# DeltaNet stage of a hybrid trunk: chunks prepared for both directions from one set of scores, decay rows fetched in a deeper ring, second inverse begun before the recurrence

## The chip, the core and the metric

One Trainium2 chip, one core of it. The engines in the profile are PE (TensorE), DVE (VectorE), ACT (ScalarE), POOL (GpSimd) and SP (SyncE, which here only issues DMAs); ACT also issues DMAs, from the same queue of instructions as its arithmetic. The metric is the device time of one execution in microseconds, the median of several runs.

## The reference, cut to what matters

One layer of a trunk with four branches, cross attention and a mixture of experts over 1024 tokens of width 1024. The change lies in branch D, the bidirectional gated DeltaNet with 4 heads of width 64:

```
def gdn_scan(q, k, v, beta, log_a):
    ...
    gam = jnp.cumsum(gc, axis=-1)
    diff = gam[..., :, None] - gam[..., None, :]
    ...
    decay = jnp.exp(jnp.where(incl, diff, -jnp.inf))
    kk = jnp.einsum('bhntd,bhnsd->bhnts', kc, kc)
    a_mat = jnp.where(strict, bc[..., None] * kk * decay, 0.0) + jnp.eye(c, dtype=jnp.float32)
    rhs = jnp.concatenate([vc * bc[..., None], kc * (bc * jnp.exp(gam))[..., None]], axis=-1)
    sol = lax.linalg.triangular_solve(a_mat, rhs, left_side=True, lower=True, unit_diagonal=True)
    u_val, k_cum = sol[..., :dv], sol[..., dv:]
    qk = jnp.einsum('bhntd,bhnsd->bhnts', qc, kc) * decay
    ...
    def step(state, inp):
        u_i, kc_i, qk_i, qd_i, kd_i, cd_i = inp
        v_new = u_i - jnp.einsum('bhtd,bhde->bhte', kc_i, state)
        o = jnp.einsum('bhtd,bhde->bhte', qd_i, state) + jnp.einsum('bhts,bhse->bhte', qk_i, v_new)
        state = cd_i[..., None, None] * state + jnp.einsum('bhsd,bhse->bhde', kd_i, v_new)
        return state, o
...
    o_f = gdn_scan(q, k, v, beta[:, :, 0], log_a[:, :, 0])
    o_b = _flip(gdn_scan(_flip(q), _flip(k), _flip(v), _flip(beta[:, :, 1]), _flip(log_a[:, :, 1])))
```

The scan runs once forward and once backward. The products of keys with keys and of queries with keys inside one chunk do not depend on the direction; the decays and the write strengths beta do.

## The kernel before

The kernel works in chunks of 128 tokens, TT = 8 of them. One list, `schedule` (made in `plan_schedule`), orders the work of all engines. Every engine walks the same list and carries out its own part of each step, so the list fixes each engine's order, and semaphores hold the engines together. `dense` lays the parts of the dense projections (a part is six 128x512 matmuls of L800, or twelve of 128x256) into a list of other steps: each `None` in that list is one part. The dense work between the DeltaNet steps belongs to branch 2's merge and the gates of branch 3 (panels `merge20` to `merge23`, `early1`, `early2`, `nz`). With a panel go its conversions (L1355 on ACT, L1971 on DVE) and the evacuations of its groups: a gate group is evacuated by ACT (L1381), an "up" group by DVE (L1994, L2000). Two PSUM banks alternate for them, so a group waits until the group two before it has been evacuated.

DeltaNet is done in two stages, each over eight indices i.

Preparation. Index i stands for chunk i in the forward direction and for chunk 7 - i in the backward one. Part 0: the rows of the summed log decays come back from DRAM (`gdn_rows`, broadcast to 128 partitions, one DMA for each direction, issued by ACT at L1728 two indices ahead), POOL takes the differences and masks them (L2823, L2826), ACT takes the exponential into the buffer that will be written out (L1722). That buffer, `LQ[i % 2]`, must have been written to `gdn_lq` for index i - 2 first, and ACT waits for that. Part 1: PE forms the scores, 8 matmuls for each direction (16 instructions, L997); DVE multiplies decay by beta (L2393) and both by the scores (L2401, twice for each direction). Part 2: ACT copies the diagonal 32x32 blocks aside (L1734, eight small copies), and `gdn_out` issues the write of 1 MB to `gdn_lq` (L1769).

The diagonal blocks of four indices (128 of them: four indices, two directions, four heads, four blocks) are sent to DRAM (`gdn_ship`, L1773), come back with one block in each of 128 partitions (`gdn_read`, L1783), and are inverted there by DVE, one row at a time: 30 rows, each a multiplication (L2413) and a subtraction (L2416), cut into ten steps `gdn_inv` of three rows, called p = 0 to 9 below. L2408 opens it, L2419, L2421 and L2424 close it. There are two such inverses, b = 0 for indices 0 to 3 and b = 1 for 4 to 7. `gdn_back` writes the inverse to DRAM (L1789), `gdn_load_inv` fetches the piece for an index (L1809, four DMAs), and `gdn_load` fetches the prepared matrices (L1799).

Recurrence (`gdn_c`, parts 0 to 6 for each index). POOL spreads the inverse into block diagonals (L2835, four instructions) and scales the keys (L2853, L2855). Two doubling steps complete the triangular inverse: PE L1021, DVE L2434, PE L1030 and L1037, DVE L2439 and L2441, PE L1021, ACT L1753, PE L1037, ACT L1757. Then PE L1044, ACT L1761, PE L1050 and L1058, DVE L2447, PE L1064 to L1072, ACT L1765, DVE L2452 and L2457.

In the list before, five of the ten steps of inverse 0 stand between the preparations of indices 5 to 7 and five after them; all ten steps of inverse 1 stand between the parts of the recurrence for indices 0, 1 and 2. Where a wait of a DMA stands in ACT's queue, everything behind it on ACT waits too, evacuations of gates among it.

## Time and profile before

| | us |
|---|---|
| median of 3 runs | 2031.6 |
| lowest, highest | 2030.33, 2033.76 |
| the profiled execution's own time | 2035.94 |
| its span in the trace | 2034.2 |

PE is busy for 1883.2 us of the span (93%), DVE for 1384.7 (68%), ACT for 1078.3 (53%), POOL for 312.2 (15%); the mean granted clock of TensorE is 0.971 of full speed. The profiled execution's time is 1.7 us above its span and 4.3 us above the median. The preparation, the inverses and the recurrence lie between 676.57 us (first L997) and 954 us (last L1072), 14% of the span. Timeline rows give start, duration, engine, line, operation and in brackets the idle time of that engine ahead of it with what ended it; ACTq is ACT's sequencer issuing a DMA.

### The profile page before, as it was taken

To read this page: it belongs to the slowest core of one execution; us is meant where nothing else is said; L and a number is where in the kernel's file an instruction comes from. 1 tells how busy PE (TensorE), PEld (TensorE's weight loads), DVE (VectorE), ACT (ScalarE), POOL (GpSimd) and SP (SyncE) were. 2 spreads that over 40 slices of the span, in tenths; PEclk is the share of its full clock that TensorE was granted. 3 is DMA by queue.
4 is the path that set the end of the run, shared out by engine and by line. 5 is a ranking of instruction groups with operands and counts; after the bars stand their busy time and mean duration, and the time that the engine had idled before them with its cause. 6 is when DMAs were issued, how large, how long until landed. Compare 5 with 4: busy or idle time off the path is not lost.

```text
span 2034.2 us, 32665 instructions
## 1 busy us (share of the span) xinstructions
PE 1883.2 (93%) x12949; PEld 1118.7 (55%) x12949; DVE 1384.7 (68%) x1833; ACT 1078.3 (53%) x1568; POOL 312.2 (15%) x269
## 2 busy tenths in 40 slices
PE   6999999999999989899999999995899999999991
PEld 3464565655544545677488855684455444444440
DVE  5555533799874797544733745437799999999997
ACT  4563223566646531223433534334588888888873
POOL 6000100344310502241000000000000111111103
PEclk8999999999999999999999999997899999999996
DMA  5411111212011663431621410404799999999987
GB/s 189 162 48 46 32 42 48 73 48 58 22 28 47 198 195 84 146 113 45 212 70 60 158 32 16 169 32 163 279 423 422 422 422 422 422 422 422 423 328 269
DMA packets 145821, 366.83 MB, mean 180 GB/s; under 512 B 39296, under 2 KB 94880, under 8 KB 119072
## 3 DMA queue, kind: packets, MB, share of 16 engines
q1 hardware_dynamic: 96608, 279.57, 36.2%
q10 hardware_dynamic: 40240, 52.50, 7.6%
q0 software_dynamic: 8848, 33.03, 4.3%
q8 instruction: 86, 1.41, 0.3%
q14 instruction: 39, 0.32, 0.0%
HBM read 314.14 MB, written 46.73 MB: 177 GB/s over the span
## 4 chain that ended last, share of the span: by engine, by line
PE 77%; DVE 8%; ACT 5%; issue 4%; DMA 3%; ACTq 1%; SPq 1%; POOL 1%; POOLq 0%; DVEq 0%
PE psum L800 38%; PE psum L1191 24%; ACT arena L1637 2%; PE psum L1180 1%; DMA gdn_lq<-arena 1%; PE psum L1115 1%; PE psum L1090 1%; DVE arena L2314 1%; PE psum L930 1%; PE psum L1209 1%; PE psum L817 1%; ACTq L1809 1%; PE psum L1072 1%; PE psum L1050 1%; DMA arena<-in_w_in_dram 1%
## 5 line engine op out<-in xcount | busy, mean ns | idle before, releaser
L800 PE MATMUL psum<-arena 128*128 128x512 f16 (+2 forms) x6000 | 1017.2, 327 | 18.3 <-ACT arena L1381 6.9
L800 PEld LDWEIGHTS psum<-arena 128*128 128x128 f16 x6000 | 569.1, 99 | 402.0 <-issue 19.2
L1191 PE MATMUL psum<-arena 128*128 128x512 f16 x2304 | 513.6, 382 | 15.2 <-issue 12.2
L751 DVE SCALAR_TENSOR_TENSOR arena<-arena 128x2048 f16<-128x2048 f32 x192 | 437.4, 2286 | 57.0 <-ACT arena L745 56.8
L745 ACT ACTIVATE arena<-arena 128x2048 f16<-128x2048 f32 x192 | 365.4, 1908 | 71.1 <-DMA arena<-in_w_dram 41.9
L1191 PEld LDWEIGHTS psum<-arena 128*128 128x128 f16 x2304 | 224.6, 98 | 282.0 <-issue 24.3
L1971 DVE SCALAR_TENSOR_TENSOR arena<-arena 128x512 f16<-128x512 f32 (+1 forms) x185 | 125.6, 698 | 114.9 <-ACT arena L1355 114.5
L2872 POOL DMA_INDIRECT arena<-xhat,arena x32 | 66.5, 2078 | 841.5 <-PE psum L1180 445.2
L1355 ACT ACTIVATE arena<-arena 128x512 f16<-128x512 f32 (+1 forms) x212 | 127.4, 616 | 53.5 <-PE psum L800 21.7
L1381 ACT ACTIVATE arena<-psum,arena 128x512 f32<-128x512 f32 x60 | 41.0, 684 | 139.4 <-PE psum L800 138.6
L1444 ACT ACTIVATE arena<-psum 128x512 f32<-128x512 f32 (+3 forms) x51 | 29.9, 586 | 127.6 <-PE psum L800 127.6
L1409 ACT ACTIVATE arena<-arena 128x256 f32<-128x256 f32 x64 | 26.7, 416 | 109.8 <-DVE arena L2006 108.7
L2767 POOL TENSOR_SCALAR arena<-arena 128x512 f32<-128x512 f32 x27 | 57.5, 2130 | 137.7 <-ACT arena L1355 137.7
L2299 DVE CUSTOM_DVE_ANT_0 arena<-psum,arena 128x1024 f32<-128x1024 f32 x64 | 75.6, 1219 | 1.8 <-PE psum L917 1.7
L1637 ACT ACTIVATE arena<-arena 128x1024 f32<-128x1024 f32 x64 | 72.9, 1146 | 6.8 <-DVE arena L2299 6.7
L1994 DVE SCALAR_TENSOR_TENSOR arena<-arena,psum 128x512 f32<-128x512 f32 x64 | 43.8, 684 | 43.2 <-PE psum L800 32.2
L2024 DVE SCALAR_TENSOR_TENSOR arena<-psum,arena 128x512 f16<-128x512 f32 x36 | 24.9, 690 | 61.2 <-ACT arena L1444 31.0
L2006 DVE SCALAR_TENSOR_TENSOR arena<-psum,arena 128x512 f32<-128x512 f32 x32 | 22.1, 691 | 65.0 <-PE psum L800 65.0
L1646 ACT ACTIVATE arena<-psum 128x512 f16<-128x512 f32 x64 | 34.7, 595 | 55.1 <-PE psum L930 34.3
L2835 POOL TENSOR_TENSOR arena<-arena 128x512 f32<-128x512 f32 x32 | 34.5, 1110 | 146.4 <-PE psum L1058 94.4
L1886 ACT ACTIVATE arena<-psum 128x512 f32<-128x512 f32 x64 | 38.2, 597 | 15.3 <-PE psum L1191 14.6
L1180 PE MATMUL psum<-arena 128*128 128x128 f32 x256 | 34.5, 279 | 9.4 <-DMA arena<-xhat,arena 9.4
(388 smaller groups left out, 2020.6 us busy)
## 6 DMA issues: line engine op xcount, KB each, us to landing
arena<-in_w_dram SPq DMA_DIRECT2D x192, 1024.0 KB, 11.9
arena<-in_merge_w_dram SPq DMA_DIRECT2D x64, 256.0 KB, 3.2
yrows<-arena ACTq DMA_DIRECT2D x32, 512.0 KB, 7.8
arena<-in_w_in_dram SPq DMA_DIRECT2D x48, 256.0 KB, 2.8
gdn_lq<-arena ACTq DMA_DIRECT2D x8, 1024.0 KB, 4.5
arena<-gdn_lq ACTq DMA_DIRECT2D x8, 1024.0 KB, 4.9
arena<-in_xattn_wkv_dram SPq DMA_DIRECT2D x32, 256.0 KB, 2.9
yrows<-arena POOLq DMA_DIRECT2D x1, 7680.0 KB, 24.1
```

What stands on the lines that cost most here:

```text
L745: nc.scalar.activation(half_of(pieces(e, m)[0], half), half_of(XLAND[m], half), ACT.Copy, scale=WS).then_inc(w_hi[m], 1)
L751: nc.vector.scalar_tensor_tensor(half_of(lo, half), half_of(XLAND[m], half), WS, half_of(hi, half), ALU.mult, ALU.subtract).then_inc(w_lo[ ...
L800: mm = nc.tensor.matmul(bank[prt[0]:prt[1], c0:c1], lhs[a](k), rhs[b](k), start=(k == 0 and a + b == 0), stop=(k == nk - 1 and a == 1))
L1180: tr = nc.tensor.transpose(PS[:, k // 4, (k % 4) * P:(k % 4) * P + P], xs[:, k, :], ident)
L1191: mm = nc.tensor.matmul(PS[:, bank, :], left[a][:, k, :], right[b][:, k, columns], start=k + a + b == 0, stop=(k == n - 1 and a == 1))
L1355: S.activation(W[i % 2][0][:, 2 * j:2 * j + 2, 0:wide], LAND[c % NLAND][:, :, 0:wide], ACT.Copy, scale=WS).then_inc(*act_hi.mark(c))
L1637: S.activation(DS[u % 2][:, m, :], DS[u % 2][:, m, :], ACT.Exp, scale=-1.0, bias=d_mx[u % 2][:, m:m + 1], accum_out=d_l[u % 2][:, m:m + 1])\
L1971: V.scalar_tensor_tensor(W[i % 2][1][:, 2 * j:2 * j + 2, 0:wide], LAND[c % NLAND][:, :, 0:wide], WS, W[i % 2][0][:, 2 * j:2 * j + 2, 0:wid ...
L1994: V.scalar_tensor_tensor(dst, gate, 1.0, bank, ALU.add, ALU.mult).then_inc(*e.mark(n))
L2299: V.tensor_tensor_reduce(out=DS[u % 2][:, m, :], in0=PS[:, 2 + 2 * m:4 + 2 * m, :].rearrange("p a b -> p (a b)"), in1=DWH[:, 896 - P * qt: ...
L2767: G.tensor_scalar(landed_c, landed_c, WS, None, ALU.mult).then_inc(*counter("pool_w_scaled").mark(chunk))
L2872: G.indirect_dma_start(XR[e % 2], None, XH_D, bass.IndirectOffsetOnAxis(IDX[:, e:e + 1], 0)).then_inc(rows_in[e % 2], 16)
```

## The change

An index of the preparation now stands for one chunk in both directions. The order of chunks is CH = 0, 7, 1, 6, 2, 5, 3, 4, so that index i (with i ^ 1 for the other direction) holds what the recurrence's index needs. The scores are formed once for each chunk, and two sets of PSUM banks alternate by i % 2. The rows of both directions come in one DMA of 512 KB for each chunk. The buffers of rows from index 2 on form a ring of three; rows 2 and 3 are issued at the start of index 0, rows j = i + 3 at `gdn_out(i)`, with four semaphores. ACT's exponential works in place in the rows' buffer, so it no longer waits for the write of `gdn_lq`; DVE waits for that write ahead of its first product instead. The 1 MB write is two DMAs of 512 KB. Inverse pieces are grouped by chunk: four DMAs write an inverse where two did, and two DMAs fetch a piece where four did. In the list, p = 0 and 1 of inverse 0 stand in the preparation and p = 2 to 9 behind it; p = 0 to 5 of inverse 1 stand ahead of the recurrence and p = 6 to 9 in its index 0, followed by `gdn_back(1)` ahead of part 6. The `None` entries are set anew: three dense parts for each index of the preparation instead of three or four, and from index 3 of the recurrence on every dense part stands where it stood.

```diff
@@ -260,19 +260,20 @@
     inv = lambda b, p: [("gdn_inv", b, 3 * p + 1, 3 * p + 4)]
     gdn += [("gdn_a", 0, 0), None, None, None, None]
     for i in range(TT):
-        mid = {6: inv(0, 2)}.get(i, [])
-        gdn += [("gdn_a", i, 1)] + {6: inv(0, 1), 7: inv(0, 4)}.get(i, []) + [None] + [("gdn_a", i + 1, 0), None] * (i + 1 < TT) + mid
-        gdn += [("gdn_a", i, 2), ("gdn_out", i)] + [("gdn_ship", 0)] * (i == 3) + [None]
-        gdn += {4: [("gdn_read", 0), None], 5: inv(0, 0) + [None], 6: inv(0, 3) + [None], 7: [("gdn_ship", 1)]}.get(i, [])
-    for p in range(5, 10):
-        gdn += inv(0, p) + [None] * (2 + (p < 8)) + [("gdn_load", p - 5)] * (p < 7)
-    gdn += [("gdn_back", 0)] + [None] * 6 + [("gdn_load_inv", 0), ("gdn_load_inv", 1), ("gdn_read", 1)] + [None] * 7
+        gdn += [("gdn_a", i, 1), None] + [("gdn_a", i + 1, 0), None] * (i + 1 < TT) + [("gdn_a", i, 2), ("gdn_out", i)]
+        gdn += {3: [("gdn_ship", 0)], 5: inv(0, 0), 6: inv(0, 1), 7: [("gdn_ship", 1)]}.get(i, []) + [None]
+        gdn += {4: [("gdn_read", 0)], 7: [None]}.get(i, [])
+    for p in range(2, 10):
+        gdn += inv(0, p) + [None] * (2 + (p == 9)) + {5: [("gdn_read", 1)], 6: [("gdn_load", 0)], 7: [("gdn_load", 1)]}.get(p, [])
+    gdn += [("gdn_back", 0)]
+    for p in range(6):
+        gdn += inv(1, p) + [None, None] + [("gdn_load_inv", 0), ("gdn_load_inv", 1)] * (p == 2)
     for i in range(TT):
         for part in range(7):
-            gdn += [("gdn_back", 1)] * ((i, part) == (3, 1))
-            gdn += [("gdn_c", i, part)] + [None] * (1 + (i < 3 and part in (1, 4) and (i, part) != (2, 1)))
-            if i < 3 and part in (1, 2, 4) or (i, part) == (0, 5):
-                gdn += inv(1, 3 * i + (i > 0) + (1, 2, 4, 5).index(part))
+            gdn += [("gdn_back", 1)] * ((i, part) == (0, 6))
+            gdn += [("gdn_c", i, part), None] + [None] * (i < 2 and part in (1, 4))
+            if i == 0 and part in (1, 2, 4, 5):
+                gdn += inv(1, 6 + (1, 2, 4, 5).index(part))
             if part == 2 and i and i + 1 < TT:
                 gdn += [("gdn_load", i + 1), ("gdn_load_inv", i + 1)]
...
-        NGR = [[f32(BR + 8192 + 1024 * j + 512 * d, NH, P) for d in range(2)] if j < 2 else (NX, NZ_)[j % 2] for j in range(TT)]
+        NGR = [f32(BR + 8192 + 1024 * j, 2, 512) if j < 2 else f32(UN + 2048, 2, 1536)[:, :, 512 * (j % 3):512 * (j % 3) + 512]
+               for j in range(TT)]
+        NDT = [[m[:, d, :].rearrange("p (h n) -> p h n", h=NH) for d in range(2)] for m in NGR]
+        CH = [c for k in range(TT // 2) for c in (k, TT - 1 - k)]
+        AT = [CH.index(i) for i in range(TT)]
...
-                    for d in range(2):
-                        c = i if d == 0 else TT - 1 - i
-                        cs = slice(c * P, c * P + P)
-                        B0, B1, B2 = (PS[:, 2 + 3 * d + b, :].rearrange("p (h n) -> p h n", h=NH) for b in range(3))
-                        if part == 1:
-                            if i == 0 and d == 0:
-                                pe.wait_ge(*counter("act_gdnp").at("tm", "nv", 3))
-                                pe.wait_ge(*counter("act_gdnp").at("egrows"))
-                            if i:
-                                pe.wait_ge(*v.at("qt", i - 1, d))
-                            for t in range(4):
-                                for u, bank in enumerate((B1, B2)):
-                                    hp = slice(64 * u, 64 * u + 64)
-                                    mm = nc.tensor.matmul(bank[:, t, :], NK[hp, t % 2, cs], (NK if t < 2 else NQ)[hp, t % 2, cs],
-                                                          start=True, stop=True)
-                                    if t == 3:
-                                        mm.then_inc(*q.mark("qk", i, d, u))
+                    cs = slice(CH[i] * P, CH[i] * P + P)
+                    B1, B2 = (PS[:, 3 + 3 * s + b, :].rearrange("p (h n) -> p h n", h=NH) for b in range(2))
+                    if part == 1:
+                        if i == 0:
+                            pe.wait_ge(*counter("act_gdnp").at("tm", "nv", 3))
+                            pe.wait_ge(*counter("act_gdnp").at("egrows"))
+                        if i >= 2:
+                            pe.wait_ge(*v.at("qt", i - 2, 1))
+                        for t in range(4):
+                            for u, bank in enumerate((B1, B2)):
+                                hp = slice(64 * u, 64 * u + 64)
+                                mm = nc.tensor.matmul(bank[:, t, :], NK[hp, t % 2, cs], (NK if t < 2 else NQ)[hp, t % 2, cs],
+                                                      start=True, stop=True)
+                                if t == 3:
+                                    mm.then_inc(*q.mark("qk", i, u))
...
                     if part == 0:
+                        for j in range(2, 4) if i == 0 else ():
+                            act.wait_ge(*counter("act_gdnp").at("tm", "nv", 3))
+                            S.dma_start(NGR[j], A["gdn_rows"][0].rearrange("(d c h) n -> c d (h n)", d=2, h=NH)[CH[j]].partition_broadcast(P))\
+                                .then_inc(gam_in[j % 4], 16)
                         for d in range(2):
-                            c = i if d == 0 else TT - 1 - i
                             act.wait_ge(*po.at("low", i, d))
-                            after(act, lq_out[i % 2], 16 * (i // 2))
-                            S.activation(NQT[i % 2][d], NGR[i][d], ACT.Exp).then_inc(*a.mark("dt", i, d))
-                        j = i + 2
-                        for d in range(2):
-                            if j < TT:
-                                act.wait_ge(*(a.at("dt", j - 2, d) if j >= 4 else counter("act_gdnp").at("tm", "nv", 3)))
-                                r0 = 32 * d + 4 * (j if d == 0 else TT - 1 - j)
-                                S.dma_start(NGR[j][d], A["gdn_rows"][0, r0:r0 + 4].partition_broadcast(P)).then_inc(gam_in[j % 2], 16)
+                            S.activation(NDT[i][d], NDT[i][d], ACT.Exp).then_inc(*a.mark("dt", i, d))
                     elif part == 2:
...
                     act.wait_ge(*counter("vec_gdn").at("qt", i, 1))
-                    S.dma_start(A["gdn_lq"][i], LQ[i % 2]).then_inc(lq_out[i % 2], 16)
+                    j = i + 3
+                    if 4 <= j < TT:
+                        S.dma_start(NGR[j], A["gdn_rows"][0].rearrange("(d c h) n -> c d (h n)", d=2, h=NH)[CH[j]].partition_broadcast(P))\
+                            .then_inc(gam_in[j % 4], 16)
+                    for d in range(2):
+                        S.dma_start(A["gdn_lq"][i ^ d, :, 1024 * d:1024 * d + 1024], LQ[i % 2][:, 1024 * d:1024 * d + 1024]).then_inc(lq_out[i % 2], 16)
...
                     for n, m in enumerate((NU[b], NUT[b])):
-                        S.dma_start(A["gdn_inv"][b, n].rearrange("u (b f) -> (u b) f", b=4), m.rearrange("p r c -> p (r c)")).then_inc(inv_out[b], 16)
+                        for d in range(2):
+                            S.dma_start(A["gdn_inv"][b, n].rearrange("(k e h) (b f) -> e k (h b) f", e=2, h=NH, b=4)[d],
+                                        m[64 * d:64 * d + 64].rearrange("p r c -> p (r c)")).then_inc(inv_out[b], 16)
...
-                    S.dma_start(LQ[s], A["gdn_lq"][i]).then_inc(lq_in[s], 16)
+                    S.dma_start(LQ[s], A["gdn_lq"][AT[i]]).then_inc(lq_in[s], 16)
                 elif what == "gdn_load_inv":
                     i = step[1]
                     s = i % 2
-                    act.wait_ge(inv_out[i // 4], 32)
+                    b, k = divmod(AT[i], 4)
+                    act.wait_ge(inv_out[b], 64)
                     if i >= 2:
                         act.wait_ge(*counter("pe_gdn").at("o", i - 2, 1))
                     for n in range(2):
-                        for d in range(2):
-                            u0 = 16 * d + 4 * (i % 4)
-                            S.dma_start(XZC[s][:, 8 * n + 4 * d:8 * n + 4 * d + 4, :],
-                                        A["gdn_inv"][i // 4, n, u0:u0 + 4].rearrange("u (p c) -> p u c", c=32)).then_inc(lq_in[s], 16)
+                        S.dma_start(XZC[s][:, 8 * n:8 * n + 8, :],
+                                    A["gdn_inv"][b, n, 8 * k:8 * k + 8].rearrange("u (p c) -> p u c", c=32)).then_inc(lq_in[s], 16)
...
                             if i >= 2:
                                 dve.wait_ge(*a.at("diag", i - 2, d, 3))
-                            V.tensor_tensor(NLT[s][d], NQT[s][d], bc(BES[:, d, c, :].unsqueeze(2), P, NH, P), ALU.mult)\
+                                dve.wait_ge(lq_out[s], 32 * (i // 2))
+                            V.tensor_tensor(NLT[s][d], NDT[i][d], bc(BES[:, d, CH[i], :].unsqueeze(2), P, NH, P), ALU.mult)\
                                 .then_inc(*v.mark("dt1", i, d))
                             dve.wait_ge(*v.last())
-                            BB = PS[:, 3 + 3 * d:5 + 3 * d, :]
+                            BB = PS[:, 3 + 3 * s:5 + 3 * s, :]
                             for u in range(2):
-                                dve.wait_ge(*q.at("qk", i, d, u))
-                            for n, (of, to) in enumerate((("lt", NLT), ("qt", NQT))):
-                                both = to[s][d].rearrange("p (u t) n -> p u (t n)", u=2)
-                                V.tensor_tensor(both, BB[:, :, 256 * n:256 * n + 256], both, ALU.mult).then_inc(*v.mark(of, i, d))
+                                dve.wait_ge(*q.at("qk", i, u))
+                            for n, (of, to, by) in enumerate((("lt", NLT[s][d], NLT[s][d]), ("qt", NQT[s][d], NDT[i][d]))):
+                                to, by = (m.rearrange("p (u t) n -> p u (t n)", u=2) for m in (to, by))
+                                V.tensor_tensor(to, BB[:, :, 256 * n:256 * n + 256], by, ALU.mult).then_inc(*v.mark(of, i, d))
```

ACT's queue in the preparation, from the write at the end of index 0 to the conversion behind index 1's write. L1769 and L1773 are `gdn_out`, L1722 and L1726 the exponential, L1728 and L1770 the fetch of rows, L1734 and L1733 the diagonal copies. Before:

```order
L1769 DMA gdn_lq<-arena 128x2048
L1381 ACTIVATE arena<-psum,arena 128x512
L1722 ACTIVATE arena<-arena 128x512 x2
L1728 DMA arena<-gdn_rows 128x512 x2
L1734 ACTIVATE arena<-arena 32x128 x8
L1769 DMA gdn_lq<-arena 128x2048
L1355 ACTIVATE arena<-arena 128x512
```

Now:

```order
L1773 DMA gdn_lq<-arena 128x1024 x2
L1384 ACTIVATE arena<-psum,arena 128x512
L1726 ACTIVATE arena<-arena 128x512 x2
L1733 ACTIVATE arena<-arena 32x128 x8
L1770 DMA arena<-gdn_rows 128x2x512
L1773 DMA gdn_lq<-arena 128x1024 x2
L1358 ACTIVATE arena<-arena 128x512
```

The fetch of rows moved behind the diagonal copies and stands directly ahead of the two writes.

DVE's queue ahead of the first product of the recurrence (L2434 before, L2438 now). L2421, L2424 close inverse 0; L2417, L2420 are rows of an inverse in the changed kernel. Before:

```order
L2421 TENSOR_SCALAR arena<-arena 128x1024
L2424 MEMSET arena 128x32 x2
L1971 SCALAR_TENSOR_TENSOR arena<-arena 128x512
L1994 SCALAR_TENSOR_TENSOR arena<-arena,psum 128x512
...
L1971 SCALAR_TENSOR_TENSOR arena<-arena 128x512 x2
L1994 SCALAR_TENSOR_TENSOR arena<-arena,psum 128x512
L2000 TENSOR_TENSOR arena<-arena 128x512
L2434 TENSOR_SCALAR arena<-psum 32x4x32 x4
```

Now:

```order
L1976 SCALAR_TENSOR_TENSOR arena<-arena 128x512
L1999 SCALAR_TENSOR_TENSOR arena<-arena,psum 128x512
L2005 TENSOR_TENSOR arena<-arena 128x512
L2417 TENSOR_TENSOR arena<-arena 128x240
L2420 TENSOR_TENSOR arena<-arena 128x15x16
L2417 TENSOR_TENSOR arena<-arena 128x238
L2420 TENSOR_TENSOR arena<-arena 128x14x17
L2417 TENSOR_TENSOR arena<-arena 128x234
L2420 TENSOR_TENSOR arena<-arena 128x13x18
L2438 TENSOR_SCALAR arena<-psum 32x4x32 x4
```

Eighteen rows of inverse 1 now stand between the end of inverse 0 and the first product of the recurrence; the last three are shown.

ACT's queue from the copy ahead of L1050 (L1761 before, L1760 now) in index 0 of the recurrence to the fetch of rows for index 1. Before:

```order
L1761 ACTIVATE arena<-psum 128x256 x2
L1355 ACTIVATE arena<-arena 128x512
L1381 ACTIVATE arena<-psum,arena 128x512
L1765 ACTIVATE arena<-psum 128x256 x2
L1748 DMA arena<-gdn_rows 64x256 x4
```

Now:

```order
L1760 ACTIVATE arena<-psum 128x256 x2
L1384 ACTIVATE arena<-psum,arena 128x512
L1794 DMA gdn_inv<-arena 4x16x1024 x4
L1764 ACTIVATE arena<-psum 128x256 x2
L1747 DMA arena<-gdn_rows 64x256 x4
```

The four writes of inverse 1 now stand ahead of the copies that free the output's bank for index 1.

## Rows read from the trace of the kernel before

**Rows 1.** The chain that ended last: by engine, page.

```profile
PE 77%; DVE 8%; ACT 5%; issue 4%; DMA 3%; ACTq 1%; SPq 1%; POOL 1%; POOLq 0%; DVEq 0%
```

**Rows 2.** Timeline of PE: start, duration, line, idle ahead and its releaser.

```profile
676.57 2.06 PE L997 MATMUL psum<-arena 64*128 64x128 f32 x32
...
717.03 5.35 PE L800 MATMUL psum<-arena 128*128 128x512 f16 x24
...
746.11 28.87 PE L800 MATMUL psum<-arena 128*128 128x512 f16 x126 [6.15 <-DVE arena L1994]
...
802.20 0.60 PE L1021 MATMUL psum<-arena 32*32 32x32 f32 x32
...
805.16 0.34 PE L1030 MATMUL psum<-arena 32*32 32x32 f32 x5 [0.95 <-DVE arena L2434]
...
814.74 1.09 PE L1044 MATMUL psum<-arena 128*64 128x128 f32 x16 [1.07 <-ACT arena L1757]
...
838.42 1.09 PE L1044 MATMUL psum<-arena 128*64 128x128 f32 x16 [2.35 <-ACT arena L1757]
...
861.79 1.98 PE L1044 MATMUL psum<-arena 128*64 128x128 f32 x16 [1.99 <-ACT arena L1757]
```

**Rows 3.** Waits in 665 to 760 us: who, for whom, total, times, longest.

```profile
ACT arena L1722 <- DMA gdn_lq<-arena: 15.2, 6, 3.7
```

**Rows 4.** Stretch, us, busy of PE, PEld, DVE, ACT, POOL; clock, DMA share, GB/s.

```profile
678.64:780.58 101.94, 87.53 (x571) 44.97 (x572) 81.36 (x146) 40.60 (x99) 29.86 (x30) 0.95 0.63 196
850.98:874.62 23.64, 21.66 (x227) 14.75 (x226) 7.24 (x22) 4.88 (x11) 6.41 (x9) 0.93 0.43 134
874.62:894.59 19.97, 19.97 (x227) 13.85 (x227) 9.25 (x25) 4.58 (x10) 7.30 (x9) 1.00 0.49 153
862.00:867.00 5.00, 5.00 (x34) 3.49 (x33) 1.36 (x3) 1.54 (x4) 0.00 (x0) 0.68 0.72 185
```

**Rows 5.** Timeline of DVE.

```profile
663.65 1.29 DVE L1971 SCALAR_TENSOR_TENSOR arena<-arena 128x512 f16<-128x512 f32 x2
...
776.15 2.81 DVE L1971 SCALAR_TENSOR_TENSOR arena<-arena 128x512 f16<-128x512 f32 x2 [6.15 <-ACT arena L1355]
...
780.59 1.24 DVE L2434 TENSOR_SCALAR arena<-psum 32x128 f32<-32x128 f32 x4
...
786.61 1.03 DVE L2408 COPY arena<-arena 64x1024 f32<-64x1024 f32 x1
787.67 0.20 DVE L2413 TENSOR_TENSOR arena<-arena 128x30 f32<-128x30 f32 x1
...
796.20 0.42 DVE L2447 TENSOR_TENSOR arena<-psum,arena 128x256 f32<-128x256 f32 x1 [0.85 <-PE psum L1058]
```

**Rows 6.** DVE: rows of inverse 1 (L2413, then L2416), p = 0 to 5.

```profile
786.61:815.55 28.94, 6.17 (x18) 1.00 0.17 54
786.61:815.55 28.94, 6.21 (x18) 1.00 0.17 54
```

**Rows 7.** DMA issues in 676 to 743 us: KB each, median us to landing.

```profile
gdn_lq<-arena ACTq DMA_DIRECT2D x8, 1024.0 KB, 4.5
arena<-gdn_diag ACTq DMA_DIRECT2D x2, 256.0 KB, 6.6
```

**Rows 8.** Timeline of ACT and its DMA issues (ACTq).

```profile
705.12 1.30 ACT L1734 ACTIVATE arena<-arena 32x128 f32<-32x128 f32 x4 [0.41 <-ACT arena L1722]
...
835.45 2.50 ACTq L1809 DMA_DIRECT2D arena<-gdn_inv  x4
...
852.24 2.21 ACTq L1789 DMA_DIRECT2D gdn_inv<-arena  x2
```

**Rows 9.** Timeline of POOL.

```profile
773.94 4.48 POOL L2835 TENSOR_TENSOR arena<-arena 128x512 f32<-128x512 f32 x4 [52.05 <-DMA arena<-gdn_inv]
...
794.91 4.04 POOL L2835 TENSOR_TENSOR arena<-arena 128x512 f32<-128x512 f32 x4 [13.30 <-PE psum L1058]
803.08 0.61 POOL L2853 TENSOR_TENSOR arena<-arena 128x256 f32<-128x256 f32 x1 [4.14 <-DVE arena L2457]
```

30 lines of the change are left out of this document (14 added, 16 removed).

## The prediction

> **What bounds the kernel now.** I read the chain of work that ended last first: PE holds 77% of it [rows 1], so a wait of PE is lost unless PE waits again later for the same thing. Then the timeline of PE, from the first scores at 676.57 us to the recurrence's index 4 at 874.62. PE's large wait is the 6.15 us at 746, for an evacuation by DVE; in the recurrence it waits 0.95 us for DVE and 1.07, 2.35 and 1.99 us for ACT's L1757 [rows 2]. Third, the list of waits: in the preparation ACT waits 15.2 us in six waits for writes to gdn_lq, with evacuations of gates queued behind [rows 3]. That is what the in-place exponential removes. Fourth, busy time by stretch: between DVE's first product of the preparation (678.64) and its first of the recurrence (780.58), DVE is busy for 81.36 of 101.94 us and PE for 87.53 [rows 4]. So DVE has only some 20 us of room there, and the change moves 18 rows of inverse 1 into it. From index 4 of the recurrence on PE has no idle time (19.97 busy of 19.97 us, rows 4), so what is gained by then reaches the end.
>
> **The scores.** 128 of 256 instructions of L997 go. 32 of them stand in 2.06 us [rows 2], so 8 x 1.0 = 8 us of PE's work goes. I cost it at nothing: it lies ahead of the first product of the recurrence, and there DVE comes last, as the next part shows. If DVE were early, it would be worth up to 8 us.
>
> **When DVE reaches the recurrence.** Everything DVE does before L2434 remains: 81.36 us busy [rows 4]. Of it I take off 1.5 us, the lengthening of two L1971 (2.81 us for two, against 1.29 without POOL beside them, rows 5) that I count again under POOL. The 60 instructions of inverse 0 leave gaps of 0.03 us each (786.61 + 1.03 to 787.67, rows 5): 1.8 us. The moved steps p = 0 to 5 are 6.17 + 6.21 us of rows [rows 6] and 1.03 us of L2408 [rows 5], with 37 such gaps: 14.5 us. Without a wait DVE arrives at 678.64 + 81.36 - 1.5 + 1.8 + 14.5 = 774.8.
>
> Waits in the preparation: the write of index i - 2 now holds DVE instead of ACT. A write lands 4.5 us after its issue [rows 7]; a fetch of rows of 512 KB is now issued right ahead of it, and diagonal copies of 1.30 us stand ahead of both [rows 8]. DVE's own work on the index between, about 4.4 us plus conversions, covers most of that. What is not covered is the conversion on DVE (L1971), which needs ACT's L1355, which stands behind the last diagonal copies (1.3 us) and three issues. Walking the two queues index by index, I find DVE idle for 2.1, 1.2 and 1.2 us ahead of three conversions, and 0.9 us for the first inverse's blocks, which need 6.6 us to land [rows 7]: 5.4 us. Bounds 0 (writes and conversions all covered) and 14 us (each of six indices also waits 1.5 us, because the write shares the DMAs with the rows in front of it). DVE then arrives at 780.2.
>
> POOL: the four L2835 and the four scalings of keys for index 0 now run while DVE works on inverse 1. Their length is 4 x 1.01 (4.04 for four) + 4 x 0.61 = 6.5 us [rows 9]. The nearest row is the pair of L1971 at 776.15: beside POOL's L2835 until 778.42 it took 2.81 us instead of 1.29, 1.52 us lost in 2.27 us of POOL [rows 5, 9], a share of 0.67. Rows of an inverse read two operands from SBUF as L1971 does, and about 85% of DVE's instructions there are such: 6.5 x 0.67 x 0.85 = 3.7 us. Bounds 0 and 6.5. I take 3.7 since the row is the same kind of instruction beside the same line. The Trainium skill ("SBUF — State Buffer", Who interferes with whom) says that a DVE instruction with two SBUF inputs and a GpSimd instruction that reads SBUF exclude each other, and that the later one blocks until the other's end. By that rule it would be nearer 6.5; it speaks against this change, and is weighed as a rival.
>
> So DVE reaches the recurrence at 783.9, 3.3 us later than before (780.59, rows 5), and PE's L1030 waits for it. PE's own work to that place is 87.53 - 8 + 1.3 (a part more, below) = 80.8 us, so that it could be there from 759.5 on, and inverse 0, which the first product needs, ends earlier than before. **Term 1: +3.3 us.**
>
> **The recurrence.** Term 2: one dense part that stood in indices 0 to 2 now stands ahead, where PE has room. Four parts take 5.35 us [rows 2]: -1.3 us.
> Term 3: indices 0 to 2 hold p = 6 to 9 instead of all ten. The 0.95 us for DVE goes. The waits for L1757 (1.07, 2.35) come from ACT issuing four L1809, 2.50 us for four [rows 8]; two are left, 1.2 us less, and in index 2 a gate's evacuation no longer stands right ahead of them. I keep 0.4: -4.0 us. Bounds -4.4 and -1 (if an issue of twice the blocks takes twice as long).
> Term 4: p = 9 and the end of inverse 1 (3.6 us, an estimate: three short pairs of rows and two instructions of the size of L2408) stand on DVE behind L2447 of index 0, and on ACT the four writes of `gdn_back(1)` wait for it, ahead of the copies L1765 (L1764 now) that free PE's bank for index 1. From POOL's L2835 of index 1 (794.91, when PE's L1058 is done) to index 1's start (802.20) there were 7.3 us. Now: 1.7 to the end of L2447 (796.20 + 0.42, rows 5), 3.6, issues of 2.0 (0.4 to 1.1 each: 2.21 for two at 852.24, rows 8) and copies of 0.8: 8.1, a wait of 0.9 (0.8 rounded up for the gaps). POOL's L2835 stands beside it for 2.2 us more: 1.4. +2.3 us, bounds 0 and 5.
> Term 5: index 3 took 23.64 us where index 4 took 19.97 [rows 4] with the same work. 1.99 us were the wait for L1757, and the rest the clock, 0.68 granted in the 5 us behind that wait. With 1.2 us fewer issues most of the wait goes; -2.0, bounds 0 and -3.6.
>
> Sum: +3.3 - 1.3 - 4.0 + 2.3 - 2.0 = -1.7 us. The profiled execution would take 2035.94 - 1.7 = 2034.2, and the median 2031.6 - 1.7 = 2029.9. The profiled run lay 4.3 us above the median, so only the difference is carried over.
>
> **Rivals.**
> A, POOL costs nothing and DVE enters early. For it: DVE's products from PSUM beside POOL keep their length. Then 3.7 and 1.4 us go from terms 1 and 4: -6.8, 2024.8. With the preparation's waits at 0 too it would be -12.2, 2019.4.
> B, slower: DVE and POOL exclude each other fully. Place: p = 3 to 5 ahead of the recurrence and the end of inverse 1. Price: 2.8 more in term 1, 2.6 more in term 4, and after some 5 us of waiting PE's clock stays low for a while as in index 3: 1.6. -1.7 + 7.0 = +5.3, 2036.9. (The rule of the Trainium skill named above is this rival.) It decides from about 0.95 us lost for each us of POOL, together with that clock. Against it: the measured share is 0.67.
> C, the writes: each of the six indices from 2 on waits 1.5 us more behind the 512 KB of rows, +9 less what other waits hide (1.3): -1.7 + 7.7 = +6.0, 2037.6. Against it: the DMA engines were 63% busy over the stretch [rows 4], so there is room.
> D, the change doesn't fetch earlier: rows j = i + 3 are issued behind the copies of index i, where rows i + 3 stood just ahead of them before. POOL's wait stays, ACT's exponential comes late, +2: 2031.9. POOL's work for an index (4 x 1 us) starts two indices ahead, which speaks against a cost.
>
> **How the numbers follow.** The measurement can tell about 0.2%, 4.1 us, from no change. The forecast has a chance of 0.40, with a range of its own of 2025.5 to 2034.5; of it 0.10 is faster by more than that, 0.25 within, 0.05 slower. A has 0.34 (0.27 faster, 0.07 same), B 0.14 (0.11 slower, 0.03 same), C 0.08 (0.06 slower, 0.02 same), D 0.04 (same). Faster 0.37, same 0.41, slower 0.22. The range runs from A's far half to B and most of C: 2020.5 to 2037.5.
>
> **What would show it.** In the profile after: ACT's wait for gdn_lq is gone and DVE has one; the last product of the preparation ends near 732 by the same walk; DVE's first product of the recurrence starts at 784 (A: 780 or less, B: 787), with PE waiting for it; L2835 lies beside rows that take longer than 0.4 us; PE waits about 2 us at index 1's start and hardly for L1757; index 4 starts at 873. It is wrong if PE reaches the recurrence later than DVE, or if the waits in the preparation pass 10 us.

## The result, and the profile after

The changed kernel takes 2046.96 us (median of 6 runs, 2045.52 to 2048.83) against 2032.68 for the kernel before in the same comparison. The ratio is 1.0071, 95% interval 1.0056 to 1.0086: 14 us slower, where the prediction said 2029.9 and a range of 2020.5 to 2037.5.

The profiled execution of the kernel after took 2045.59 us, span 2043.8, granted clock 0.971. PE still holds the chain (78%, where [rows 1] had 77%), so the loss has to be found as waits of PE. First its timeline, to be laid beside [rows 2]: start, duration, line, idle ahead and its releaser. L1000 are the scores (L997 before), L1024 the start of an index of the recurrence (L1021), L1033 the product that waits for DVE (L1030).

```profile
676.24 1.16 PE L1000 MATMUL psum<-arena 64*128 64x128 f32 x16
...
722.62 2.74 PE L805 MATMUL psum<-arena 128*128 128x512 f16 x6 [5.64 <-ACT arena L1384]
...
772.88 7.93 PE L805 MATMUL psum<-arena 128*128 128x512 f16 x30 [3.86 <-ACT arena L1384]
786.15 5.54 PE L805 MATMUL psum<-arena 128*128 128x512 f16 x18 [5.33 <-ACT arena L1384]
...
795.10 0.34 PE L1033 MATMUL psum<-arena 32*32 32x32 f32 x5 [1.48 <-DVE arena L2438]
...
815.68 0.71 PE L1067 MATMUL psum<-arena 128*128 128x128 f32 x4 [2.77 <-DVE arena L2451]
...
825.00 0.71 PE L1024 MATMUL psum<-arena 32*32 32x32 f32 x32 [2.61 <-issue]
...
849.12 0.60 PE L1024 MATMUL psum<-arena 32*32 32x32 f32 x32
...
869.19 0.60 PE L1024 MATMUL psum<-arena 32*32 32x32 f32 x32
...
890.14 0.60 PE L1024 MATMUL psum<-arena 32*32 32x32 f32 x32
```

The first scores stand at 676.24 (676.57 before), index 4 at 890.14 (874.62 before): 15.5 us are lost in between, and the split is clean. DVE's first product of the recurrence comes at 794.43 instead of 780.59 [rows 5]: +13.8. From there to index 1's start it is 825.00 - 794.43 = 30.57 us, where it was 802.20 - 780.59 = 21.61: +9.0. Indices 1 to 3 take 890.14 - 825.00 = 65.14 us instead of 72.42: -7.3. Of the 30.57 us PE works for 24.49, at a granted clock of 0.89, where it worked for all of the 21.61 at full clock: 6.1 of the 9.0 us are PE standing idle and 2.9 are matmuls lengthened by the lower clock (columns: us, busy of PE, PEld, DVE, ACT, POOL, granted clock, share of the 16 DMA engines, GB/s; first the kernel before, then the kernel after, then a part of it and one of the groups made longer).

```profile
780.59:802.20 21.61, 21.61 (x204) 14.40 (x202) 17.55 (x46) 4.93 (x11) 5.05 (x6) 1.00 0.12 36
```

```profile
794.43:825.00 30.57, 24.49 (x200) 16.26 (x201) 22.34 (x54) 4.08 (x10) 6.74 (x8) 0.89 0.09 26
816.00:820.00 4.00, 4.00 (x24) 4.00 (x23) 3.63 (x13) 0.00 (x0) 0.00 (x0) 0.57 0.01 4
```

```profile
816.84 1.81 PE L1075 MATMUL psum<-arena 128*128 128x64 f32 x8
```

What lies behind index 4 is not changed; it measures between 1153.7 and 1160.4 us from execution to execution of all the kernels here, which is why the two profiled spans differ by 9.6 and the medians by 14.3.

Where do the 13.8 us come from? DVE's timeline (as rows 5), with every wait of over half a us between the first product of the preparation (678.48) and the recurrence:

```profile
689.76 0.69 DVE L1976 SCALAR_TENSOR_TENSOR arena<-arena 128x512 f16<-128x512 f32 x1 [0.85 <-ACT arena L1358]
...
696.45 0.90 DVE L1976 SCALAR_TENSOR_TENSOR arena<-arena 128x512 f16<-128x512 f32 x1 [2.15 <-ACT arena L1358]
...
704.39 0.69 DVE L1976 SCALAR_TENSOR_TENSOR arena<-arena 128x512 f16<-128x512 f32 x1 [1.29 <-ACT arena L1358]
...
714.16 0.69 DVE L1976 SCALAR_TENSOR_TENSOR arena<-arena 128x512 f16<-128x512 f32 x1 [4.46 <-ACT arena L1358]
...
723.75 1.03 DVE L2412 COPY arena<-arena 64x1024 f32<-64x1024 f32 x1 [3.27 <-DMA arena<-gdn_diag]
...
749.46 0.69 DVE L1999 SCALAR_TENSOR_TENSOR arena<-arena,psum 128x512 f32<-128x512 f32 x1 [0.93 <-PE psum L805]
...
786.71 0.99 DVE L1976 SCALAR_TENSOR_TENSOR arena<-arena 128x512 f16<-128x512 f32 x1 [4.43 <-ACT arena L1358]
...
789.07 1.24 DVE L2417 TENSOR_TENSOR arena<-arena 128x240 f32<-128x240 f32 x1
790.34 1.13 DVE L2420 TENSOR_TENSOR arena<-arena 128x240 f32<-128x240 f32 x1
791.50 0.70 DVE L2417 TENSOR_TENSOR arena<-arena 128x238 f32<-128x238 f32 x1
...
794.43 1.24 DVE L2438 TENSOR_SCALAR arena<-psum 32x128 f32<-32x128 f32 x4
```

The waits shown make 17.4 us; with three short ones (0.18, 0.38, 0.23) it is 18.2. Without POOL beside it a row of this length takes about 0.4 us; at 789 to 790 two take 1.24 and 1.13, the next four 0.7 each. The next timeline, of ACT and its DMA issues (ACTq) and of POOL, shows who was waited for at 782 to 787, and again at 825:

```profile
709.74 2.71 ACTq L1770 DMA_DIRECT2D arena<-gdn_rows  x1
...
766.99 5.04 ACTq L1794 DMA_DIRECT2D gdn_inv<-arena  x4
772.14 0.69 ACT L1384 ACTIVATE arena<-psum,arena 128x512 f32<-128x512 f32 x1 [10.40 <-DVE arena L2420]
...
783.03 2.28 ACTq L1814 DMA_DIRECT2D arena<-gdn_inv  x4
785.40 0.69 ACT L1384 ACTIVATE arena<-psum,arena 128x512 f32<-128x512 f32 x1 [12.06 <-issue]
...
819.49 4.98 ACTq L1794 DMA_DIRECT2D gdn_inv<-arena  x4
824.52 0.38 ACT L1764 ACTIVATE arena<-psum 128x256 f32<-128x256 f32 x1 [16.15 <-issue]
```

```profile
786.12 5.09 POOL L2839 TENSOR_TENSOR arena<-arena 128x512 f32<-128x512 f32 x4 [64.68 <-DMA arena<-gdn_inv]
```

The four writes of the inverse are issued in 5.04 us (1.3 each; in the kernel before the two writes at the same place took 0.81 together, and the two of inverse 1 took 2.21 [rows 8]), and ACT can issue the loads behind them only at 783.03, 11 us after the last: it stands on their landing, with a gate's evacuation and a conversion behind it. In the kernel before the writes were issued at 764.76 and POOL spread the blocks from 773.94 [rows 9]; now it is 766.99 and 786.12. The stretches below (columns as above) show how the writes travel: the first is the kernel after behind the issues, the second the kernel before behind its writes.

```profile
772.00:778.00 6.00, 5.12 (x18) 2.11 (x19) 5.41 (x14) 1.21 (x2) 0.00 (x0) 0.72 0.26 101
```

```profile
764.80:769.50 4.70, 4.70 (x24) 2.14 (x22) 2.62 (x5) 0.69 (x1) 0.00 (x0) 1.00 0.83 279
```

A DMA share of 0.26 at 101 GB/s stands against 0.83 at 279. In the second write, of inverse 1, the issues of 4.98 us stand right ahead of ACT's copies L1764, which free PE's bank for index 1 (825.00, the 2.61 us "issue").

### The profile page after: what moved, and what is told of

Its sections match the earlier page's. It is cut to its first block, busy times and chain, and to the rows that moved or that the text cites. A ratio compares the mean times of both kernels' runs of the same rounds, so it can differ in the third digit from the quotient of the medians.

```text
span 2043.8 us, 32387 instructions
## 1 busy us (share of the span) xinstructions
PE 1879.4 (92%) x12821; PEld 1112.0 (54%) x12821; DVE 1385.4 (68%) x1833; ACT 1078.8 (53%) x1568; POOL 308.0 (15%) x269
## 4 chain that ended last, share of the span: by engine, by line
PE 78%; DVE 8%; ACT 5%; issue 4%; DMA 3%; ACTq 1%; SPq 1%; POOL 1%; DVEq 0%; POOLq 0%
PE psum L805 39%; PE psum L1194 24%; ACT arena L1640 2%; PE psum L1183 1%; PE psum L1093 1%; PE psum L1118 1%; DVE arena L2319 1%; PE psum L935 1%; PE psum L1212 1%; PE psum L1075 1%; PE psum L822 1%; DMA gdn_inv<-arena 1%; PE psum L1053 1%; DMA gdn_diag<-arena 1%; PE psum L946 1%
## 5 line engine op out<-in xcount | busy, mean ns | idle before, releaser
L1194 PEld LDWEIGHTS psum<-arena 128*128 128x128 f16 x2304 | 224.5, 98 | 282.2 <-issue 24.4
L2839 POOL TENSOR_TENSOR arena<-arena 128x512 f32<-128x512 f32 x32 | 34.6, 1110 | 160.3 <-PE psum L1061 82.2
## 6 DMA issues: line engine op xcount, KB each, us to landing
yrows<-arena POOLq DMA_DIRECT2D x1, 7680.0 KB, 24.1
```

What stands on the lines that cost most here:

```text
L1194: mm = nc.tensor.matmul(PS[:, bank, :], left[a][:, k, :], right[b][:, k, columns], start=k + a + b == 0, stop=(k == n - 1 and a == 1))
```

## The experiments

In the table below the last three columns are in us after the first scores matmul of the same execution. "Product" is DVE's first of the recurrence, the next two the starts of index 1 and index 4 on PE. The median stands beside the ratio to the kernel before (with its interval), whose own medians were 2031.4 to 2032.7. The ratio is not the quotient of the two medians, and the two can differ by some 3 us: e3 is 19.6 us above the kernel before by medians and 16 by its ratio, and e7 is 3.9 us below e1 by medians and 7 by the ratios. So a difference of 2 or 3 us between two medians decides nothing by itself. The positions, taken from one profiled execution of each kernel, are free of what lies behind index 4, and they carry the argument.

```
kernel               median   ratio (95%)               product  index 1  index 4
before               2032.7   1                           104.0    125.6    198.0
after                2047.0   1.0071 (1.0056-1.0086)      118.2    148.8    213.9
e1_whole             2041.8   1.0054 (1.0034-1.0073)      111.8    139.9    207.2
e2_flat4             2045.2   1.0062 (1.0041-1.0083)      113.9    142.4    209.5
e3_before_split      2051.1   1.0079 (1.0056-1.0103)      114.3    136.3    220.3
e4_whole_back_later  2043.6   1.0058 (1.0040-1.0076)      115.0    143.1    208.4
e5_out_later         2041.4   1.0048 (1.0034-1.0062)      112.2    140.0    207.3
e6_five_ahead        2051.0   1.0084 (1.0058-1.0110)      112.1    141.7    216.9
e7_no_spread         2037.9   1.0018 (1.0002-1.0033)      111.6    135.5    201.5
e8_scores_twice      2043.0   1.0049 (1.0032-1.0065)      115.3    143.1    210.1
e9_inv0_later        2038.2   1.0037 (1.0024-1.0050)      108.7    136.6    201.8
e10_rows_part3       2040.5   1.0035 (1.0021-1.0049)      115.0    139.4    204.8
e11_loads_later      2042.1   1.0061 (1.0039-1.0082)      114.6    142.6    205.5
e12_all_four         2035.3   1.0015 (0.9999-1.0031)      108.4    132.8    195.5
e13_loads_split      2032.3   1.0001 (0.9986-1.0015)      107.8    132.3    195.1
e14_five_again       2035.0   1.0008 (0.9995-1.0022)      106.5    130.5    200.6
e15_before_loads     2027.0   0.9973 (0.9958-0.9988)      104.5    126.2    191.6
```

Eight kernels with the same preparation (after, e1, e2, e4, e6, e7, e10, e11) put the last product of the preparation at 59.0 to 62.0, so a front that differs by under 3 us between two of them says nothing; e1 is the early one.

**The write of the inverse.** The loss shown first was tested from both sides: e1 takes the new form out of the kernel after, e3 puts it into the kernel before.

```
# e1 (with the reads in four pieces of 64 KB, as before)
-                        for d in range(2):
-                            S.dma_start(A["gdn_inv"][b, n].rearrange("(k e h) (b f) -> e k (h b) f", e=2, h=NH, b=4)[d],
-                                        m[64 * d:64 * d + 64].rearrange("p r c -> p (r c)")).then_inc(inv_out[b], 16)
+                        S.dma_start(A["gdn_inv"][b, n].rearrange("u (b f) -> (u b) f", b=4), m.rearrange("p r c -> p (r c)")).then_inc(inv_out[b], 16)
```

> The kernel after, with the inverse written as in the kernel before: each half (U, UT) in one transfer of 512 KB from 128 partitions to one contiguous block, and read back in four pieces of 64 KB per index. Nothing else differs. Theory M (the way the inverse is written is the loss): in the kernel after the four transfers by direction have an outermost dimension of 4, keep the DMA share at 0.26 from 772 to 778 us and land 11 us after the last issue; ACT waits for them until 783.0, its gate evacuations and POOL's spreading behind. Written whole, ACT's load issue goes to about 772, POOL's L2839 starts at 776 instead of 786.1, DVE's 4.4 us wait for the conversion at 782 goes, and in index 0 the 5.0 us of issues ahead of the copies L1764 shrink to 1 to 2 us: 4.4 + 3 to 4, so 7 to 9 us faster than the kernel after, 2038 to 2040. Theory O (the order is the loss: DVE's rows moved ahead of the recurrence and beside POOL): the write is covered by other work; 0 to 2 us faster than the kernel after, 2045 to 2047.

```
# e2, against e1: again four writes, but each to one contiguous block
+                        for d in range(2):
+                            S.dma_start(A["gdn_inv"][b, n, 16 * d:16 * d + 16].rearrange("u (b f) -> (u b) f", b=4),
+                                        m[64 * d:64 * d + 64].rearrange("p r c -> p (r c)")).then_inc(inv_out[b], 16)
```

> As e1_whole, but each half is still written in two transfers by direction (256 KB from 64 partitions each, four in all as in the kernel after), now to contiguous blocks. Theory M1 (what costs is the outermost dimension of 4, which leaves most DMA engines without work): like e1_whole within 2 us (two issues of 0.4 us more each time), 2038 to 2041, with a DMA share near 0.8 behind the write. Theory M2 (what costs is the number of transfers, 1.25 us of issue each, and 64 partitions in each): as the kernel after within 2 us, 2045 to 2048, with L1794 still at 5 us for four.

e3 is the kernel before with the removed lines of e1's diff in place of its one write; it still reads four pieces for each index.

> The kernel before with one edit: the inverse is written in the four transfers by direction of the kernel after (to a layout in which both directions of an index stand together), and read back in the same four pieces per index. Theory M: the load issue of ACT goes from 769.5 to about 780, POOL's spreading from 773.9 to 786, and PE's first product of the recurrence waits for it: +7 to +10; the second write stands in index 3, where 5 us of issues instead of 2.2 stand ahead of L1753, and ACT waits for its landing ahead of index 3's loads: +5. In sum 10 to 16 us slower than the kernel before, 2042 to 2048. Theory O: up to 2 us slower.

e1 is 5.1 us faster than the kernel after (7 to 9 expected), e3 19.6 slower than the kernel before (10 to 16 expected; 16 by its ratio). Part of e1's earlier product is its early front. Counted from the end of inverse 0 (766.91 and 764.56), DVE's product comes after 27.5 us in the kernel after and 24.0 in e1, and index 0 takes 30.6 and 28.1: the form of the write is worth 3.5 us ahead of the recurrence and 2.5 in index 0. The issues and landings, e1, e2, then e3 (its L1790 is the write, L1811 the read, L1381 the evacuation):

```profile
764.64 0.81 ACTq L1793 DMA_DIRECT2D gdn_inv<-arena  x2
...
768.58 5.43 ACTq L1814 DMA_DIRECT2D arena<-gdn_inv  x8
```

```profile
768.26 2.82 ACTq L1794 DMA_DIRECT2D gdn_inv<-arena  x4
773.81 5.65 ACTq L1816 DMA_DIRECT2D arena<-gdn_inv  x8
```

```profile
765.81 5.19 ACTq L1790 DMA_DIRECT2D gdn_inv<-arena  x4
...
780.84 4.28 ACTq L1811 DMA_DIRECT2D arena<-gdn_inv  x8
```

```profile
787.77 2.74 PE L800 MATMUL psum<-arena 128*128 128x512 f16 x6 [9.25 <-ACT arena L1381]
...
884.90 1.97 PE L1044 MATMUL psum<-arena 128*64 128x128 f32 x16 [9.85 <-ACT arena L1757]
```

From the first issue to the first load it is 3.9 us in e1, 5.6 in e2, and 15.0 to 16.0 in e3 and after. Two transfers more cost 1.6 us (e2), the strided destination some 10 more. While they travel, the DMA share is 0.62 in e1 and 0.69 in e2 (244 and 202 GB/s, over stretches of some 5 us from the first issue), and 0.26 in e3 and after. The share fits four of sixteen engines, and 4 is the outermost dimension of the strided form. The Trainium skill ("DMA: Bandwidth & Descriptors", Rules for kernel authors) states just that: a transfer whose slowest dimension has fewer than 16 steps is confined to at most that many engines. The trace agrees, 0.26 against 0.69, though it does not show the engines one by one. By its median alone (2045.2, spread 2040.6 to 2049.7) e2 falls into the range of M2 (2045 to 2048) and not of M1 (2038 to 2041); its interval overlaps that of e1. It is the traces that speak for M1: four issues in 2.82 us and not 5, the landing 10 us earlier than in the kernel after, the share of 0.69, and an index 4 only 2.3 us behind e1's, with a product as late as its later front explains. One reason why e1 gained less than expected in full are its four reads per index, which cost ACT more: index 3 took 24.5 us instead of 20.9, with 2.86 us of PE's waiting for L1756 behind 3.0 us of issues.

**The copies of index 0.** e4 is e1 with one position changed:

```
-            gdn += [("gdn_back", 1)] * ((i, part) == (0, 6))
+            gdn += [("gdn_back", 1)] * ((i, part) == (1, 0))
```

> As e1_whole, and the second inverse's write is issued one step later on ACT, behind the copies of index 0's outputs (L1764) instead of ahead of them. If the end of inverse 1 on DVE holds those copies and with them index 1's first product (in the kernel after PE stands 2.6 us ahead of it, and ACT's copies come right behind the four issues that end at 824.5): 2 to 4 us faster than e1_whole. If PE's index 1 waits for something else there (POOL's spreading, DVE's state): within 1 us of e1_whole.

No gain (median 1.7 us above e1's): from the product to index 1 it is 28.1 us in both. With issues of 0.8 us the copies are not what index 1 waits for; the 2.61 us in the kernel after were the issues, which e1's 2.5 us shorter index 0 agrees with.

**DVE beside POOL.**

```
# e7, against e1
                     def spread(dst, of, d):
+                        if i < 2:
+                            return G.tensor_tensor(dst[:, 0:1, 0:32], XZC[s][:, 0:1, :], bc(blk_of[:, 0:1].unsqueeze(1), P, 1, 32), ALU.mult)
```

> As e1_whole (2041.8), but POOL's spreading of the inverse's blocks (L2839) is left out for indices 0 and 1: each of its four instructions handles 32 columns instead of 512, so that two indices of the recurrence compute on other data. All waits stay. In e1_whole DVE's rows beside POOL took 0.69 to 1.2 us instead of 0.40: 7.7 us for 3.6 us of work ahead of the recurrence, and 4.1 for 1.2 in index 0. Theory B (DVE and POOL exclude each other while both read SBUF, and DVE is last in both places): 3 to 4 us earlier at the recurrence and 2.5 to 3 in index 0, 5 to 7 us faster than e1_whole, 2035 to 2037. Theory A (the lengthened rows are covered by other waits): 0 to 2 us faster, 2040 to 2042.

```
# e10, against e1
-            if i == 0 and part in (1, 2, 4, 5):
-                gdn += inv(1, 6 + (1, 2, 4, 5).index(part))
+            if i == 0 and part in (1, 2, 3, 5):
+                gdn += inv(1, 6 + (1, 2, 3, 5).index(part))
```

> As e1_whole (2041.8), with the rows p = 8 of inverse 1 one part earlier in index 0 (after part 3 instead of part 4). In e1 DVE waited 2.33 us for a gate's evacuation, then made these rows beside POOL's L2839 (4.1 us for 1.8 us of work), and PE waited 2.77 us for L2451 behind them. Theory B (the overlap with POOL costs, not the rows): the rows fall into DVE's wait, PE's 2.77 us go and index 0 is 2.5 to 4 us shorter (28.1 us in e1 from DVE's first product to index 1's start): 2038 to 2039.5. Rival: index 0 is bound by the end of inverse 1 or by POOL: within 1 us of e1.

From the end of inverse 0 to DVE's first product it is 24.0 to 24.1 us in e1, e4, e8, e10 and 21.0 in e7: the spreading costs 2.9 us there. From the product to index 1's start it is 28.1 in e1, 23.9 in e7, 24.4 in e10: 4.2 us, nearly all of which e10 saves by moving the rows p = 8 into DVE's wait. Both stretches together are Theory B's 5 to 7 us. e7's median is 3.9 us below e1's (7 by the ratios), its index 4 comes 5.7 us earlier; e10's median is 1.3 below (4 by the ratios; 2.3 to 3.8 expected), with a product 3.2 us later in e10's profiled execution, which is the spread of the front. DVE's rows of e1 in index 0 and what PE makes of it:

```profile
805.02 1.04 DVE L2420 TENSOR_TENSOR arena<-arena 128x150 f32<-128x150 f32 x1
806.09 1.01 DVE L2417 TENSOR_TENSOR arena<-arena 128x130 f32<-128x130 f32 x1
807.14 1.02 DVE L2420 TENSOR_TENSOR arena<-arena 128x130 f32<-128x130 f32 x1
808.19 0.99 DVE L2417 TENSOR_TENSOR arena<-arena 128x108 f32<-128x108 f32 x1
809.21 0.27 DVE L2420 TENSOR_TENSOR arena<-arena 128x108 f32<-128x108 f32 x1
```

```profile
810.00 0.71 PE L1067 MATMUL psum<-arena 128*128 128x128 f32 x4 [2.77 <-DVE arena L2451]
```

0.32, 0.29, 0.29 and 0.27 us of work become 1.0 each while POOL makes its four instructions of L2839 (804.67 to 809.05): one row per instruction of POOL, whatever its length.

**The scores.**

```
# e8, against e1
-                        for t in range(4):
+                        for r, t in ((r, t) for r in range(2) for t in range(4)):
...
-                                if t == 3:
+                                if (r, t) == (1, 3):
```

> As e1_whole (2041.8), with the 16 matmuls of an index's scores issued twice into the same banks, which gives PE back the 8 us that the change took from it in the preparation. If the saving is covered, since DVE comes last (PE stood still for 7.5 and 8.4 us in e1_whole ahead of the recurrence): within 1.5 us of e1_whole, and PE's waits there shorter by about 8 us in sum. If PE's work were on the path: up to 8 us slower, 2046 to 2050.

Median 1.2 us above e1's, within the 1.5 that was expected. Between the first products of preparation and recurrence PE is busy for 89.59 us instead of 83.58, DVE for 93.58 instead of 93.28: the matmuls filled PE's waits. e8's last product of the preparation comes at 63.2 us, 1.2 behind the latest of the eight kernels above, so the scores' saving is shown to be worth nothing up to about 1 us.

**The preparation's waits.**

```
# e5, against e1
-        gdn += [("gdn_a", i, 1), None] + [("gdn_a", i + 1, 0), None] * (i + 1 < TT) + [("gdn_a", i, 2), ("gdn_out", i)]
-        gdn += {3: [("gdn_ship", 0)], 5: inv(0, 0), 6: inv(0, 1), 7: [("gdn_ship", 1)]}.get(i, []) + [None]
+        gdn += [("gdn_a", i, 1), None] + [("gdn_a", i + 1, 0), None] * (i + 1 < TT) + [("gdn_a", i, 2)]
+        gdn += {5: inv(0, 0), 6: inv(0, 1)}.get(i, []) + [None, ("gdn_out", i)] + {3: [("gdn_ship", 0)], 7: [("gdn_ship", 1)]}.get(i, [])
# e9, against e5
-        gdn += {5: inv(0, 0), 6: inv(0, 1)}.get(i, []) + ...
+        gdn += {6: inv(0, 0), 7: inv(0, 1)}.get(i, []) + ...
```

> As e1_whole (2041.8), with the fetch of rows, the two writes of gdn_lq and the shipping of the diagonal blocks placed one dense part later in the preparation, so that ACT's conversion L1358 stands ahead of those issues instead of behind them. In the kernel after, DVE waits 12.2 us in six waits between its first product and its first copy of inverse 0, four of them for L1358, each of which starts only when the three issues ahead of it are made. Theory Q (ACT's queue of issues holds the conversion and with it DVE): three to four of those waits go, the last product of the preparation ends 3 to 6 us earlier after the first scores, and since DVE sets the start of the recurrence, 3 to 5 us faster than e1_whole, 2037 to 2039. Theory R (the waits are made by the DMA itself, rows and writes sharing the engines, or PE's parts come late): the waits come back one step on; within 1.5 us of e1_whole.

> As e5_out_later (2041.4), with the first two steps of inverse 0 one index later in the preparation (behind indices 6 and 7 instead of 5 and 6). In e5 DVE no longer waited for the conversions behind index 1, 2, 4 and 5, but its wait for the diagonal blocks (L2412 for gdn_diag) grew from 2.7 to 6.28 us, and the last product came only 2 us earlier than in the kernel after. Theory G (the round trip of the diagonal blocks is the next thing late): that wait goes, DVE's first product of the recurrence comes 4 to 6 us earlier than in e5 (112.2 us after the first scores), 2035 to 2038. Theory H (DVE then waits for what ACT and POOL make of the rows for indices 6 and 7, or PE or ACT become the bound of the stretch): 2040 to 2042.

e5 gains 0.4 us: Q's waits go and come back one step on, as R said. Its diagonal blocks, then e9 at the same place:

```profile
721.84 1.03 DVE L2412 COPY arena<-arena 64x1024 f32<-64x1024 f32 x1 [6.28 <-DMA arena<-gdn_diag]
```

```profile
717.62 0.85 DVE L1976 SCALAR_TENSOR_TENSOR arena<-arena 128x512 f16<-128x512 f32 x1 [3.70 <-ACT arena L1358]
```

e9 takes that wait away as well: product at 108.7, 3.5 us earlier (4 to 6 expected), median 3.2 us lower. Its last product of the preparation comes at 55.4 us, where the eight kernels above have 59.0 to 62.0. Theory G holds in the main, with 3.70 us left of the next wait. e5 and e9 together say what the preparation's waits hang on: to move ACT's issues alone gains nothing, since the diagonal blocks are then what is late; to give the blocks an index more does.

**Rows and loads in the recurrence.** e6 was meant to relieve the front by one step, e11 moves the loads behind L1756.

```
# e6, against e1
-    for p in range(6):
-        gdn += inv(1, p) + [None, None] + [("gdn_load_inv", 0), ("gdn_load_inv", 1)] * (p == 2)
+    for p in range(5):
+        gdn += inv(1, p) + [None] * (2 + (p > 2)) + [("gdn_load_inv", 0), ("gdn_load_inv", 1)] * (p == 2)
...
-            gdn += [("gdn_back", 1)] * ((i, part) == (0, 6))
...
-                gdn += inv(1, 6 + (1, 2, 4, 5).index(part))
-            if part == 2 and i and i + 1 < TT:
+                gdn += inv(1, 5 + (1, 2, 4, 5).index(part))
+            gdn += (inv(1, 9) + [("gdn_back", 1)]) * ((i, part) == (1, 1))
+            if part == (4 if i == 1 else 2) and i and i + 1 < TT:
# e11, against e1
-            if part == 2 and i and i + 1 < TT:
+            if part == 3 and i and i + 1 < TT:
```

> As e1_whole (2041.8), with five steps of inverse 1 ahead of the recurrence instead of six, one after each of the parts 1, 2, 4, 5 of index 0, and the last with its end after part 1 of index 1; its write follows there and the loads for index 2 are issued after part 4 instead of part 2. Theory D (DVE is the engine that comes last both ahead of the recurrence and in index 0, and the recurrence has room for rows, as index 1 of the kernel before had with three steps): DVE reaches its first product of the recurrence 2.6 us earlier, index 0 is shorter by about 1, index 1 up to 1.5 longer: 2 to 4 us faster than e1_whole, 2038 to 2040. Rival: the rows that leave the front cost the same where they land (PE waits for DVE in index 0 or 1 as long as it gains): 2041 to 2043.

> As e1_whole (2041.8), with the loads for the next index issued after part 3 instead of part 2, behind ACT's L1756. In e1 PE waits 2.86 us for L1756 in index 3, behind 3.0 us of four issues L1814, with a clock below full for some us after it (index 3 took 24.5 us where index 4 took 20.0). Theory I (the issues on ACT ahead of L1756): index 3 falls to 20 to 21 us and nothing else moves: 3 to 4 us faster, 2038 to 2039. Rival: the issues then hold L1760 as long, or POOL's spreading comes late for the next index: within 1 us of e1.

e6 is 9 us slower than e1, outside both expectations. Inverse 1 ended at 152.2 instead of 137.0, and its write stood in ACT's queue ahead of L1752:

```profile
829.65 1.52 PE L1040 MATMUL psum<-arena 64*64 64x64 f32 x16 [4.03 <-ACT arena L1752]
...
847.46 0.44 PE L1024 MATMUL psum<-arena 32*32 32x32 f32 x16 [1.25 <-POOL arena L2839]
```

This showed what the diff holds and the prediction had not drawn: since a chunk is prepared for both directions, indices 2 to 5 of the recurrence read the second inverse, where the kernel before first reads it at index 4. It is due two indices earlier.

In e11 index 3 takes 20.0 us, as Theory I expected, but PE waits 1.10 us for L1760 in index 4 and 0.80 for DVE at the start of index 7, and the median (2042.1) does not move, as the rival said.

> e1, e5, e9, e10 and e11 together: the inverse written whole, issues behind the conversion in the preparation, inverse 0 begun one index later, rows p = 8 after part 3, loads after part 3. If the four places are separate stretches of one path, their gains add: from 2041.8, 5 + 3 + 3.5 us, 2029 to 2032, level with the kernel before (2031.4). If they share a bound (DVE's own work up to index 1), less: 2034 to 2038.

```
# e13, against e12
-            if part == 3 and i and i + 1 < TT:
+            if part == (3 if i < 4 else 2) and i and i + 1 < TT:
# e14, against e13: e6's rows with p = 5 to 8 after parts 1, 2, 3, 5, and
+            gdn += inv(1, 9) * ((i, part) == (1, 1)) + [("gdn_back", 1)] * ((i, part) == (1, 2))
+            if part == (4 if i == 1 else 3 if i < 4 else 2) and i and i + 1 < TT:
# e15, against the kernel before: e13's line
```

> As e12_all_four (2035.3), with the loads for the next index after part 3 only in indices 1 to 3, and after part 2 from index 4 on as before. In e12 index 3 fell to 20.0 us, but indices 4 and 5 took 42.8 us together where the kernel before took 40.1: PE waited 1.1 us for L1760 and 0.8 us for DVE in the one that has the loads behind L1756. If the later place is good only where gates are evacuated: 2 to 3 us faster than e12, 2032 to 2033.5. If the gain at indices 4 and 5 is lost in index 3 again: 2035.

> As e13_loads_split, with one step of inverse 1 less ahead of the recurrence: p = 5 to 8 after parts 1, 2, 3, 5 of index 0, p = 9 and the end after part 1 of index 1, the write after part 2 of index 1 (in e6 it stood ahead of ACT's L1752 and PE waited 4.0 us), the loads for index 2 after part 4. If the rows ahead of the recurrence are the rest of the loss: DVE's first product 2.6 us earlier and index 0 about 1 us shorter, minus up to 1.6 us for POOL's spreading for index 2, which comes later: 2029.5 to 2031.5, level with the kernel before or just below. If the second inverse's due time at index 2 is the bound: PE waits for POOL's L2839 at index 2 as in e6 (2.8 us) and it is 2033 or more.

> The kernel before with one edit: the loads for the next index stand after part 3 instead of part 2 in indices 1 to 3, behind ACT's L1757. In the kernel before PE waits 1.07, 2.35 and 1.99 us for L1757 behind four issues L1809 of 2.1 to 2.5 us, and its clock is at 0.68 for 5 us in index 3. If those waits are on the path: index 1 to 3 are shorter by 1, 2 and 3.5 us, 5 to 6.5 us faster than the kernel before, 2025 to 2027. If they come back as waits for L1761 or POOL: within 2 us of it.

e12 and e13 put the repairs together. e12's 2035.3 lies where a shared bound was expected (2034 to 2038) and not where the gains add (2029 to 2032); e13 is 3.0 us faster than e12, as expected, and level with the kernel before (ratio 1.0001). e14 is 1.3 us ahead of e13 at the product and 5.5 behind at index 4, with PE waiting 1.71 us for L1756 and 1.25 and 1.55 for L2839: the due time of the second inverse is a bound, and of five and six steps ahead six are the better. The median is 2.7 us above e13's, in the range that was given for this bound. e15 is the fastest kernel here, 2027.0 us (2025 to 2027 expected), ratio 0.9973 (0.9958 to 0.9988), faster than both the kernel before and e13. Its waits for L1757 [rows 2] are gone, and index 3 takes 20.0 us:

```profile
829.59:851.09 21.50, 21.50 (x233) 14.36 (x232) 15.87 (x44) 5.46 (x12) 6.44 (x8) 1.00 0.43 123
851.09:871.10 20.01, 20.01 (x229) 13.89 (x230) 8.33 (x21) 4.77 (x11) 5.19 (x6) 1.00 0.49 159
```

With the loads placed alike, the repaired change (e13) is 3.5 us behind e15 at index 4: 3.3 at the product, 2.8 in index 0, less 2.6 in indices 1 to 3. In the medians it is 5.3. That is what remains of the change, and no order tried here removes it. PE stands for 8.34 us ahead of DVE's product in e13, and index 0 then runs at a clock of 0.89 (PE busy 22.90 us, where e15 has 21.80 at full clock). That DVE's moved rows are what holds it there is read from these rows; no run takes them out alone.

Of the 22.8 us that the kernel after has lost at the start of index 1, the runs price 6.0 as the form of the write (after against e1) and up to 7.1 as POOL's spreading beside DVE's rows (e7 against e1). The rest, some 10 us, is DVE's moved rows and the waits of the preparation together; e5 with e9 takes at least 3.6 of it back (last product at 55.4 instead of 59.0).

## Why the prediction was wrong

**What bounds it: right.** The prediction placed the decision on DVE ahead of the recurrence, with PE waiting for it and the scores' 8 us worth nothing. e8 shows that. Of its own signs of being wrong, one came: the waits in the preparation passed 10 us (12.0).

**Term 1: wrong, +13.8 instead of +3.3.** DVE came at 794.43, not 783.9. The work was not the error: without waits the prediction had 783.9 - 5.4 = 778.5, and measured are 794.43 - 18.2 = 776.2. The waits were: 18.2 us instead of 5.4. Two steps failed. The first is the walk through the preparation, 12.0 us of waits up to the first copy of inverse 0 instead of 5.4 (the walk's end of the last product was 732, measured 738.2). The waits for conversions came to 8.75 us instead of 4.5: the walk's 1.2 us behind three issues leave at most 0.4 us for each, and the fetch of rows at 709.74 took 2.71. The wait for the diagonal blocks came to 3.27 us instead of 0.9: they took 8.3 us to land where the walk has the 6.6 of [rows 7]. e9 shows that this wait was on the path; what made the landing longer is open. The 12.0 us lie inside the stated bounds (0 to 14), but the value taken was less than half of them. The second is an edit that was put at nothing ahead of the recurrence: the write of inverse 0 in four strided transfers, for which term 1 has neither an issue time nor a landing. It held ACT until 783.03, and with it the conversion (4.43 us of DVE) and POOL. e1 and e3 show it: to write it whole brings DVE's product 3.5 us nearer to the end of inverse 0, and the strided write puts 10.3 us ahead of the product in the kernel before. The rule of the Trainium skill named with e2 speaks against this edit and was not weighed: by it the 1 MB goes on at most a quarter of the engines. At a quarter of the 279 GB/s that the kernel before reaches there it would take 15 us (an estimate from that rule and this row); e3 shows 15.0 and the kernel after 16.0.

**POOL inside term 1: right in kind and about right in size.** 3.7 us were taken; e7 shows 2.9 for the spreading alone, with the scaling of keys still there, and in the kernel after DVE's instructions between 786.7 and 794.4 are 3.2 us longer than without POOL beside them. A share well under full exclusion was the right choice: e7's 2.9 us are 0.6 of the 4.89 us that the four L2839 lasted in e1. The 0.67 itself was misread: it divides by the 2.27 us of POOL's spreading, but POOL went on with its scalings at 778.38 beside the end of the pair, so that 1.52 us were lost in 2.81, a share of 0.54. The Trainium skill ("SBUF — State Buffer", Who interferes with whom) has the later of the two blocked until the other's end. The rows agree for each instruction (a row of 0.27 us takes 0.99, until POOL's ends), but between two of POOL's instructions one of DVE's gets in, and POOL's four take 5.09 us instead of 4.04: they take turns, so that DVE loses some 0.6 of POOL's time and not all. Rival B's price for term 1 (6.5) was too high. Its price for index 0 (1.4 + 2.6 = 4.0) is what e7 shows there, 4.2; but that is the place of the rows p = 8 and the clock behind PE's wait, since e10 recovers 3.7 of it with POOL's work unchanged. The total ended beyond B for other reasons.

**Term 4: wrong, +9.0 instead of +2.3.** The mechanism (end of inverse 1 and four issues ahead of the copies) is there; the issues were put at 2.0 us and took 4.98, for the same reason as above. PE stood 2.61 us. Two parts were missed. The rows p = 8 meet POOL's spreading in index 0 and PE waits 2.77 us for L2451, which e10 removes. And the clock was put at nothing outside of rival B: it falls to 0.50, the lower level of 1.2 GHz, twice in index 0, over 796 to 799 us behind PE's wait of 1.48 us for DVE's product and over 817 to 819 behind the 2.77 us, and L1075 takes 1.81 us instead of 1.00. That is the 2.9 us of longer matmuls in index 0; in the kernel before, where PE has no wait there, the clock is 1.00, the level of 2.4 GHz.

**Terms 2, 3 and 5: right.** -1.3 - 4.0 - 2.0 = -7.3 were forecast, and indices 1 to 3 are 7.3 us shorter (0.9, 3.7 and 2.7). That the sum agrees to 0.1 us is luck, since index 1 carries a part of term 4, the clock of 0.50 over 827 to 830 us behind the 2.61 us; the parts are right to about 1 us. Reads in two pieces instead of four do give ACT that time back (1.0 us of issue instead of 2.4 to 2.5), and e1, which gives it up, loses 3.6 us in index 3.

**Rivals.** C put the price on gdn_lq's writes holding DVE; its size (7.7) is near the 6.6 us by which the prediction took the preparation's waits too small, but DVE never waited for gdn_lq in the kernel after. The traffic held it in another way, through ACT's issues and the diagonal blocks. D: POOL was not late for rows. A fell with term 1. None of the four names the write of the inverse, so the range did not reach the result: a form of transfer that the trace of before does not show should have had a bound of its own, from both sides, like any other unknown cost.

## What to carry to other kernels

When a change alters the shape of a transfer, cost it as a new operation: issue time, landing, its outermost dimension, and who stands behind a wait for it in the issuing queue, even if the bytes are the same. When two halves of a computation are paired to save work, look for what becomes due earlier because of it. And in a queue that both issues transfers and evacuates, put the issues behind the evacuation that another engine is waiting for: moving one pair of loads by one part in three indices (e15) was worth 4.7 us in the median, where the 8 us of matmuls that the change removed were worth nothing.

## What the runs showed of the hardware

- A write of 256 KB from 64 partitions whose destination has an outermost dimension of 4 with a stride takes 1.3 us to issue and keeps the DMA share at 0.26 (101 GB/s); the same bytes to contiguous blocks take 0.7 us and reach 0.69. Four of the first kind land 15 to 16 us after the first issue, two contiguous ones of 512 KB were ready within 3.9.
- DVE and POOL, both with operands in SBUF, take turns instruction by instruction: beside POOL's L2839 its 1.01 us become 1.27 and DVE's 0.27 to 0.41 become 1.0 to 1.2, so the shortest of DVE's lose the largest multiple. With POOL's spreading left out (e7) DVE gains 2.9 us for 4.89 us of POOL.
- An issue on ACT's queue takes 0.3 to 0.5 us for the writes of gdn_lq and most fetches of rows, 0.5 to 0.7 for the reads of the inverse. The one fetch of rows that follows the shipping of the diagonal blocks by 5 to 7 us takes 2.5 to 3.6 us in twelve kernels (2.71 at 709.74 in the kernel after), but 1.1 in e1 and 1.3 in e8: the same line at the same place varies, and what decides it is not shown.
- PE's wait of 2.77 us in index 0 of the kernel after (to 815.68) is followed by a granted clock of 0.50, the lower level of 1.2 GHz, over 817 to 819 us, and 0.57 over 816 to 820, so that it costs more than its own length. In e1, with a wait of 8.38 us that ends at 789.23, the clock is 0.50 over 784 to 793 us, which takes in the first 4 us of work behind the wait.
